# Fetching and forming the first input pieces inside the filter stage, and one transfer for the small constants

## The reference

```
u = h * (1.0 + scale[:, None, :]) + shift[:, None, :]
proj = u @ w_in[layer] + b_in[layer]
hy_streams, hy_gate, pool_in, pool_gate = jnp.split(proj, splits, axis=-1)
```

## Time and profile before

| | |
|---|---|
| median of 3 runs | 1290.47 us (1288.97 to 1294.95) |
| profiled execution | 1286.0 us, of which the span of instructions is 1284.0 us |
| PE busy in the span | 1105.6 us, 86% |
| DVE, ACT busy | 844.5 us, 550.2 us |
| filter stage, until SP's last store is issued | 54.4 to 137.7 us |
| u made, chunks 0 to 3 multiplied | 142.1 to 205.0 us |
| rest of the values stage | 205.0 to 443 us |

### The profile page before, as it was taken

One profiled execution on the slowest core, in us unless ns is written; L12 is line 12 of the kernel. 1 busy time (PEld: TensorE's weight loads), 2 busy tenths in 40 slices (PEclk: granted clock), 3 DMA queues, 4 the chain that ended last, 5 costly groups with the idle time before them and its releaser, 6 DMA issues. The chain is left out here.

```text
span 1284.0 us, 14469 instructions
## 1 busy us (share of the span) xinstructions
PE 1105.6 (86%) x4928; PEld 855.4 (67%) x4928; DVE 844.5 (66%) x1101; ACT 550.2 (43%) x745; POOL 36.5 (3%) x40
## 2 busy tenths in 40 slices
PE   3999268999999999889999888998888555999996
PEld 0388147888888777667778666676666334788885
DVE  7599475555454638278989345639788358677776
ACT  4088342343443334247677233417676345111110
POOL 0001000000000000000000000000000024000000
PEclk8799778999999999999999999999999889999999
DMA  9778763677775445689997578768997696622221
GB/s 353 260 233 293 207 214 106 206 233 248 243 243 177 150 146 188 227 228 270 254 278 221 171 232 254 237 190 229 267 262 214 211 354 223 246 99 99 98 98 49
DMA packets 150456, 273.18 MB, mean 213 GB/s; under 512 B 20783, under 2 KB 42415, under 8 KB 148212
## 3 DMA queue, kind: packets, MB, share of 16 engines
q1 hardware_dynamic: 146789, 266.22, 65.2%
q0 software_dynamic: 3168, 5.51, 1.9%
q10 hardware_dynamic: 432, 0.60, 0.1%
HBM read 178.95 MB, written 98.57 MB: 216 GB/s over the span
## 5 line engine op out<-in xcount | busy, mean ns | idle before, releaser
L170 PE MATMUL prj_pp<-prj_uhi,prj_whi 128*128 128x512 f32 x768 | 309.7, 403 | 44.6 <-DVE prj_ulo L1176 39.7
L171 PE MATMUL prj_pp<-prj_ulo,prj_whi 128*128 128x512 f32 x768 | 305.3, 398 | 0.0
L172 PE MATMUL prj_pp<-prj_uhi,prj_wlo 128*128 128x512 f32 x768 | 305.1, 397 | 0.0
L170 PEld LDWEIGHTS prj_pp<-prj_uhi,prj_whi 128*128 128x128 f32 x768 | 147.9, 193 | 85.5 <-issue 54.1
L172 PEld LDWEIGHTS prj_pp<-prj_uhi,prj_wlo 128*128 128x128 f32 x768 | 147.4, 192 | 32.5
L171 PEld LDWEIGHTS prj_pp<-prj_ulo,prj_whi 128*128 128x128 f32 x768 | 147.8, 192 | 31.4
L170 PE MATMUL out_ps<-whl,out_yhi 128*128 128x512 f32 x256 | 102.2, 399 | 4.3 <-DVE out_ylo L2013 4.3
L1183 DVE TENSOR_TENSOR p_alo<-p_a,p_ahi 128x1024 fp32r<-128x1024 f32 x32 | 39.2, 1226 | 96.8 <-ACT p_ahi L1111 96.8
L171 PE MATMUL out_ps<-whl,out_yhi 128*128 128x512 f32 x256 | 102.1, 399 | 0.0
L172 PE MATMUL out_ps<-whl,out_ylo 128*128 128x512 f32 x256 | 101.9, 398 | 0.0
L1111 ACT ACTIVATE p_ahi<-p_a 128x1024 fp32r<-128x1024 f32 x32 | 33.9, 1060 | 128.6 <-PE p_ps L172 124.5
(11 more groups left out here) (181 smaller groups left out, 1982.2 us busy)
## 6 DMA issues: line engine op xcount, KB each, us to landing
kseq<-fs_xo SPq DMA_DIRECT2D x32, 512.0 KB, 4.3
p_a<-kseq SPq DMA_DIRECT2D x32, 512.0 KB, 4.4
kfreq<-p_out SPq DMA_DIRECT2D x32, 512.0 KB, 5.2
xseq<-p_xo SPq DMA_DIRECT2D x32, 512.0 KB, 7.3
p_a<-xseq SPq DMA_DIRECT2D x32, 512.0 KB, 5.9
p_k_re<-kfreq SPq DMA_DIRECT2D x64, 256.0 KB, 4.5
p_k_im<-kfreq SPq DMA_DIRECT2D x64, 256.0 KB, 5.3
bseq<-p_out SPq DMA_DIRECT2D x32, 512.0 KB, 5.9
```

The lines of the kernel that those rows point to most:

```text
L170: nc.tensor.matmul(out, w[0], m[0], start=start, stop=False, skip_group_check=True)
L171: nc.tensor.matmul(out, w[0], m[1], start=False, stop=False, skip_group_check=True)
L172: return nc.tensor.matmul(out, w[1], m[0], start=False, stop=stop, skip_group_check=True)
```

## The change

The six element-wise constants are put side by side on the host in one array of 128 rows and 76 columns (`t_rows`) and come in one transfer; with the table `edge` and the unit matrix `eye` there are three transfers in place of eight. The first weight tile, pieces 0 to 3 and these constants are now issued by SP inside the filter stage, between its last nine stores. ACT's `w_high(0)`, DVE's `w_low(0)` and `form_u` of pieces 0 to 3 stand at the end of the filter stage; `high_u` and `low_u` of these pieces stay in the values stage, because `uhi` and `ulo` take SBUF that the filter stage still uses. The pieces go through eight buffers: two of a new scope `xin`, `side`, a part of `cv`, and the four buffers `a` and `out` of the values stage, which wait for that use to end. The scope `xin` has 32 semaphores of its own and is left at the end of the values stage.

```diff
@@ filter_stage1, SP
             for n in range(N):
                 sp.wait_ge(evac_done[n % 2], n // 2 + 1)
                 sp.dma_start(group_rows(kseq[n % 2], fl.group(n // 2)), xo[n % 4][:, :, :]).then_inc(stored[n % 4], 16)
+                if n == N - 9:
+                    pj.load_w(sp, 0)
+                if N - 8 <= n < N - 4:
+                    pj.load_x(sp, n - (N - 8))
+                if n == N - 4:
+                    pj.load_consts(sp)
@@ DVE
             staggered(N, (window, 0), (low, 1))
+            pj.w_low(dve, 0)
+            for m in range(4):
+                pj.form_u(dve, m)
@@ ACT
-            staggered(N, (high, 0), (evac, 3))
+            def step(n):
+                if n == N - 3:
+                    pj.w_high(act, 0)
+
+            staggered(N, (high, 0), (step, 2), (evac, 3))
@@ Projection
+    def load_x(self, sp, m):
+        tc, k2 = m // 4, m % 4
+        src = self.t["t_xt"].rearrange("(k p) c -> p k c", p=P)
+        after(sp, self.ulo_done[m % 8], m // 8)
+        sp.dma_start(self.xt[m % 8][:, :, :], src[:, 2 * k2:2 * k2 + 2, tc * CH:(tc + 1) * CH]).then_inc(self.xt_in[m % 8], 16)
...
     def load_consts(self, sp):
         t = self.t
-        with self.nc.allow_non_contiguous_dma(reason="columns of small vectors"):
-            sp.dma_start(self.b_in[:, :], t["b_in"][0, :].rearrange("(k p) -> p k", p=P)).then_inc(self.consts, 16)
-            for j in range(3):
-                sp.dma_start(self.cw[:, j, :], t["conv_w"][0, j, :].rearrange("(k p) -> p k", p=P)).then_inc(self.consts, 16)
-            sp.dma_start(self.cb[:, :], t["conv_b"][0, :].rearrange("(k p) -> p k", p=P)).then_inc(self.consts, 16)
-            sp.dma_start(self.pscale[:, :], t["pool_scale"][0, :].rearrange("(k p) -> p k", p=P)).then_inc(self.consts, 16)
+        sp.dma_start(self.own[:, :], t["t_rows"][:, :]).then_inc(self.consts, 16)
         sp.dma_start(self.edge[:, :, :, :], t["t_edge"].partition_broadcast(P)).then_inc(self.consts, 16)
         sp.dma_start(self.eye[:, :], t["t_eye"][:, :]).then_inc(self.eye_in, 16)
@@ values_and_filters, SP
-            load_x(0)
-            load_x(1)
-            pj.load_w(sp, 0)
-            load_x(2)
-            load_x(3)
-            pj.load_consts(sp)
+            for m in range(4, 8):
+                pj.load_x(sp, m)
             pl.load(sp)
...
-                if step + 1 in form_at:
-                    for m in form_at[step + 1]:
-                        load_x(m)
+                if step + 2 in form_at:
+                    for m in form_at[step + 2]:
+                        pj.load_x(sp, m)
@@ DVE
                 if step in form_at:
                     for m in form_at[step]:
-                        form_u(m)
+                        if m >= 4 and m not in by_act:
+                            pj.form_u(dve, m)
                         if m >= 1:
-                            low_u(m - 1)
+                            pj.low_u(dve, m - 1)
@@ encoder_layer
+            with Scope(nc, "xin", "right") as w:
+                with Scope(nc, "flt", "right") as f:
+                    w.ring = [w.sb(f"xt{b}", [P, 2, CH]) for b in range(2)]
...
+                    pj = Projection(nc, t, u, w, scale1, shift)
+                    filter_stage1(nc, t, tabs, fl, kseq, pj)
```

More of the change, by code:

```diff
@@ L229, with __init__ @@
 class Scope:
-    def __init__(self, nc, tag):
-        self.nc, self.tag, self.ctx, self.semaphores = nc, tag, ExitStack(), []
+    def __init__(self, nc, tag, side="left"):
+        self.nc, self.tag, self.side, self.ctx, self.semaphores = nc, tag, side, ExitStack(), []
     def __enter__(self):
@@ L657, in __init__ @@
         self.eye = s.sb("eye", [P, P])
[L658 to L661, removed]
+        self.own = s.sb("own", [P, 76])
+        self.b_in = self.own[:, 0:24]
+        self.cw = self.own[:, 24:60].rearrange("p (j k) -> p j k", j=3)
+        self.cb = self.own[:, 60:72]
+        self.pscale = self.own[:, 72:76]
         self.edge = s.sb("edge", [P, 4, 2, PAD])
-        self.pp = [s.ps(f"pp{c}", [P, CH]) for c in range(2)]
+        self.xt = list(xin.ring)
+        self.xt += [self.side, self.cv[:, 2 * CH:4 * CH].rearrange("p (a b) -> p a b", a=2)]
+        self.xt_in, self.u_done, self.uhi_done, self.ulo_done = (
+            xin.sems(n, 8) for n in ("xt_in", "u_done", "uhi_done", "ulo_done"))
         self.w_in, self.consts, self.pad_set, self.eye_in = s.sem("w_in"), s.sem("consts"), s.sem("pad_set"), s.sem("eye_in")
@@ L667, in __init__, with hold_u @@
             s.sems(n) for n in ("whi_done", "wlo_done", "prj_done", "bank_read"))
+    def hold_u(self, s):
+        self.uhi = s.sb("uhi", [P, KT, L], F32R)
+        self.ulo = s.sb("ulo", [P, KT, L], F32R)
+        self.pp = [s.ps(f"pp{c}", [P, CH]) for c in range(2)]
+    def load_x(self, sp, m):
[3 more added lines that the diff above has]
+        sp.dma_start(self.xt[m % 8][:, :, :], src[:, 2 * k2:2 * k2 + 2, tc * CH:(tc + 1) * CH]).then_inc(self.xt_in[m % 8], 16)
@@ new lines, in form_u, with form_u_act @@
+    def form_u(self, dve, m):
+        dve.wait_ge(self.xt_in[m % 8], 16 * (m // 8) + 16)
+        for e in range(2):
+            k = 2 * (m % 4) + e
+            x = self.xt[m % 8][:, e, :]
+            ins = self.nc.vector.tensor_scalar(x, x, self.scale1[:, k:k + 1], self.shift[:, k:k + 1], ALU.mult, ALU.add)
+        ins.then_inc(self.u_done[m % 8], 1)
+    def form_u_act(self, act, m):
+        act.wait_ge(self.xt_in[m % 8], 16 * (m // 8) + 16)
+        for e in range(2):
+            k = 2 * (m % 4) + e
+            x = self.xt[m % 8][:, e, :]
+            ins = self.nc.scalar.activation(x, x, ACT.Identity, scale=self.scale1[:, k:k + 1], bias=self.shift[:, k:k + 1])
+        ins.then_inc(self.u_done[m % 8], 1)
@@ L997, in _ @@
         def _(sp):
[L998 to L1001, removed]
             def load_a(n):
                 if n < N:
+                    if n < 2:
+                        sp.wait_ge(pj.ulo_done[4 + n], 2)
                     after(sp, lo_done, n - 1)
@@ L2086, in encoder_layer @@
         shift = s.sb("shift", [P, KT])
-        with Scope(nc, "flt") as f:
-            fl = Filters(nc, f)
-            front(nc, t, fl, tabs, scale1, shift, rows)
-            filter_stage1(nc, t, tabs, fl, kseq)
         with Scope(nc, "prj") as u:
-            pj = Projection(nc, t, u)
-            gt = Gated(nc, u, pj, 16, 0)
             vf, sig, sp1, btw, sp2 = plan_steps(
```

83 lines of the change are left out of this document (42 added, 41 removed).

## The result

The changed kernel takes 1283.36 us (median of 6 runs, 1276.75 to 1288.8) against 1289.72 us before on the same chip: ratio 0.9947, interval 0.9923 to 0.9972. Built and timed once more it gave 0.994 (0.9916 to 0.9964). It is faster, but by 6 to 8 us where 14.6 were forecast, and the forecast time of 1276 us was 7 us too low. The profiled execution has a span of 1281.8 us where before had 1284.0.

The account below looks back on a forecast made before the run. PE was taken as the bound, its idle time before chunk 3 of the values stage as the gain: 20.6 - 4.6 - 2.0 + 0.6 = 14.6 us, 1286.0 to 1271.4, plus 4.5 for the median: 1276 us, range 1269 to 1283.

Parts of the forecast that it names:

- The start of chunk 3: Values stage: chunk 3 of the projection starts at 176.0 instead of 196.6, 20.6 us earlier.
- the constants are the larger part: Start of the values stage: of the 20.6 us gained, the constants give more than the pieces formed early.
- The end of the filter stage: Filter stage's drain of stores: 2.76 MB of added loads make the last store land 4.6 us later, bounds 1.0 to 10.3.
- Semaphores: Stage ends: the new scope's barrier 0.9 us and seven second clears 1.1 us, together 2.0 us lost, bounds 0 to 2.8.
- The clock: Chunk 3 of the values stage: takes 7.8 us instead of 8.4, gain 0.6; from gain 2.7 to loss 3.0.
- Rival D: Values stage: PE's clock stays down after the denser start; at 45 us of it 8 us slower, 1298 us; chance 0.02.
- A: Rival, filter stage: loads and stores slow each other, stage ends 10.3 us later; gain 8.9, 1282 us; chance 0.12.
- B: Rival, values stage: pieces come late, twelve take 31.6 us instead of 24.5; gain 7.5, 1283 us; chance 0.06.
- whatever brings the start of chunk 3 forward brings the end of that stage forward by as much: Values stage from chunk 3 on: PE is busy 246.9 of 248.0 us, so an earlier start is kept in full.
- The sign that the prediction itself named: Values stage: the forecast is wrong if the stage does not end 12 to 18 us earlier.
- rival C: Values stage: something other than chunk 3's start, for instance transfers, sets its end; no gain, 1292 us; chance 0.06.

Follow-up runs that it names:

- a_place_early: `a_place` with the six added transfers spread over the middle of the filter stage instead of between its last nine stores: 1273.94 us, 0.986 of the kernel before.
- a_place: The changed kernel with the projection's small tiles on the right side of SBUF, so u has its old address: 1278.69 us, 0.9896 of the kernel before.
- b_const_order: The kernel before with the constants in one transfer and u's halves allocated behind the projection's small tiles: 1290.24 us, 1.0003 of the kernel before.

## Why the prediction was wrong

- **The start of chunk 3** was forecast 20.6 us earlier, counted from the stage's first transfer; it came 20.8 earlier. The links held: the pace of 2.04 us a piece (156.77 to 158.81), no wait of DVE for a piece from there to chunk 3, chunk 0 released by the tables 7.2 us after the first transfer (forecast 8.1). The remark that the constants are the larger part was wrong: alone they gave 7.1. The other 13.7 belong to the pieces that are there already and to the longer ring of buffers, which no run tells apart.
- **The end of the filter stage** was put at +4.6 us and is +5.5 in both profiles of the changed kernel. The drain moved 378 GB/s, close to the 367 used. The sum counted bytes alone. It had no term for ACT's waits for stores, 2.10 and 1.48 us before its last two copies, where in the kernel before ACT waited 0.92 and 0.33 us, and for PE: the added loads delay stores that free the buffers, and with the loads moved away (`a_place_early`) these waits are gone and the stage is 3.9 us shorter than in `a_place`. That they make up the missing 0.9 us is likely but not shown. By the Trainium skill, "DMA: Bandwidth & Descriptors", section "Where 436 GB/s comes from", the term would by estimate have been 5.1, nearer; but its limit of some 358 GB/s is not what bound here, as the 378 GB/s over 18 us show.
- **Semaphores**, 2.0 us forecast: PE's barrier waits went from 4.8 + 1.1 to 5.7 + 1.6, that is +1.4, and in the second pair of executions +0.7.
- **The clock** did not turn against it: the rest of the values stage ran at a mean of 0.99 in both. Chunk 3 was put at 7.8 us instead of 8.4 and took 7.8. That this term came out is luck: the 8.4 was one execution's, the second execution of the kernel before has 5.6, and of the changed kernel 7.2. Rival D is out, and so is A (the first transfer at 151.33 is past the mark I had named for A, but 3.7 us of that were there before the filter stage began) and B (no wait for a piece).
- **The step that failed** is the one behind "whatever brings the start of chunk 3 forward brings the end of that stage forward by as much", and the sum's silence on all that follows: the stages behind chunk 3 were costed as unchanged because their instructions are. The change moves u from 192 to 64 bytes behind a multiple of 256, and each projection product then takes 232 instead of 227 ns. In the profiles this costs the values stage 3.5 us behind chunk 3 in both pairs of executions, and the next stage, without the barrier at its end, 1.3 and 2.3. Putting u at 192 again, in two ways, gives 1278.69 and 1277.94 us where the changed kernel had 1283.36 and 1282.59: 4.7 us on the mean, give or take 2. With this term the forecast of 1276 becomes 1280.7, with 0.9 for the filter stage 1281.6, and with 0.6 less for the semaphores 1281.0; the last 2 us lie within the runs' scatter. The sign that the prediction itself named, the values stage ending 12 to 18 us earlier, failed too: it ended 8.1 us earlier (444.58 to 436.46). It is rival C's outcome in part (a gain not kept), but not its mechanism: no transfer ended the stage, and PE was busy, longer for the same work.
- **Slips in the prediction's numbers.** The range of 1269 to 1283 us was said to hold the bounds of its terms, but those add up to 1268 to 1286. By its own shares, faster should have had 0.90 and same 0.08, not 0.91 and 0.07.

Left open: why the place within 256 bytes matters at all; what 32 bytes off a multiple of 64 do by themselves (whl moved from 224 to 192 changes both); and why the transforms' products in between, whose own tiles had not moved, went along in `b_const_order` (226.2 to 230.9 ns). Open is also what the spacing costs in the later stages. Only about half of the 2304 projection products lie in the values stage and the next. The 1104 behind them stand farther apart in the changed kernel too (232.6 ns instead of 229.4), but the stretch between 540 and 850 us, where the DMA share is about 0.8 and PE is busy for about 90% of the time, varied by up to 8 us among builds with no order by placement. So the number of products times the nanoseconds is not the loss, and the medians, not one profile's stages, carry the 4.7 us.

## What to carry to other kernels

When a change allocates, frees or reorders tiles, compare the addresses of the big moving operands before and after; a forecast that counts only instructions assumes they cost the same. Where a stage is bound by matmuls, count products over a fixed, fully busy stretch at the same granted clock in both profiles before looking for a wait. A second execution of each kernel shows which stages repeat (the tail, within 0.1 us) and which don't (chunk 3, 5.6 to 8.4 us). And loads added to a stage with spare DMA time belong in its middle, not between the last stores that its buffers wait for.

## What was not expected of the hardware

- The distance of f32r 128x512 products depends on where the moving operand starts, modulo 256 bytes: 226.6 to 227.7 ns at 192, 228.7 to 229.2 at 0, 232.1 to 232.4 at 64, 233.5 at 128 (projection, 19 profiles of 17 builds), and in the last stage 233.3 at 224 and 226.7 at 192. At the place 192 it did not depend on how far up the tile lies (2,240 to 44,480 bytes) nor on whether the weights lie below or above it (226.8 and 226.7 ns). Why is not known.
- The DMA engines moved 378 GB/s over 18 us of mixed loads and stores (367 in the changed kernel's second execution), and 337 GB/s over 50 us.
- Chunk 3's 24 products took 8.4 us at a clock of 0.63 in one execution of the kernel before and 5.6 us at 1.00 in another, after pauses that differed by 1.3 us.
- ScalarE needs 1.50 us for two 128x512 scale-and-shift passes that VectorE does in 1.00.
